# A cached page's eight chunk rows laid 16 partitions apart instead of side by side

## What is computed

```
def gather_pages(pool, page_table):
    g = pool[page_table]
    return g.reshape(page_table.shape[0], -1, 2, N_KV_HEADS, HEAD_DIM)

def compress_blocks(kv, cmp_pe, cmp_w):
    # BLOCK_CMP 32, STRIDE_CMP 16, so r = 2 and a chunk is 16 positions
    chunks = kv[:, :n_chunks * STRIDE_CMP].reshape(B, n_chunks, STRIDE_CMP, 2, N_KV_HEADS, HEAD_DIM)
    comp = 0.0
    for i in range(r):
        part = chunks[:, i:i + n_cmp] + pe[i]
        comp = comp + jnp.einsum('bnscgd,csde->bncge', part, w[:, i])
    return comp[:, :, 0], comp[:, :, 1], c_end
```

## Time and profile before

| | |
|---|---|
| median of three runs | 2737.37 us |
| lowest and highest | 2721.35 and 2755.52 us |
| the profiled execution | 2724.35 us |
| its span | 2722.6 us |
| mean granted share of TensorE's clock | 0.935 |
| PE busy | 2351.4 us, 86% of the span |
| DVE, ACT, GpSimd busy | 804.9, 559.6 and 170.2 us |
| mean rate of the DMA engines | 43 GB/s |

### The profile page before, as it was taken

How to read it: one execution, slowest core, us unless ns; L and a number is a source line. 1 busy time by engine, 2 the same in 40 slices (tenths; PEclk the granted TensorE clock), 3 DMA queues, 4 the chain that set the end, 5 groups by cost and what they waited for, 6 DMA issues and landing times.

```text
span 2722.6 us, 37448 instructions
## 1 busy us (share of the span) xinstructions
PE 2351.4 (86%) x15820; PEld 1321.1 (49%) x15820; DVE 804.9 (30%) x1750; ACT 559.6 (21%) x1292; POOL 170.2 (6%) x253
## 2 busy tenths in 40 slices
PE   8999899888874696877755589899999999999999
PEld 4464445787863573333322334454454445444543
DVE  2046333556551237765433201101110111111101
ACT  4024331222211124655512212100000000000000
POOL 2000000222201111111100000000000000000000
PEclk9998889999985897999977799899999999999999
DMA  5000003000005530000033330101011010101000
GB/s 156 17 8 23 24 16 120 3 11 11 3 4 87 98 111 1 1 1 1 23 117 109 85 141 27 62 0 62 3 59 62 0 62 0 62 0 62 0 31 35
DMA packets 84726, 115.75 MB, mean 43 GB/s; under 512 B 30899, under 2 KB 68724, under 8 KB 83406
## 3 DMA queue, kind: packets, MB, share of 16 engines
q1 hardware_dynamic: 84558, 113.35, 13.9%
HBM read 104.75 MB, written 12.64 MB: 43 GB/s over the span
## 4 chain that ended last, share of the span: by engine, by line
PE 75%; DVE 7%; DMA 5%; SPq 4%; ACT 4%; issue 3%; POOL 0%; POOLq 0%; DVEq 0%; ACTq 0%
PE psum L1121 71%; DMA arena<-in_cache_cmp_kv_dram 3%; SPq L612 2%; DVE arena L2067 2%; SPq L580 2%; PE psum L1524 1%; ACT arena L1028 1%; PE psum L1581 1%; DVE arena L1934 1%; ACT arena L1014 1%; DVE psum L2062 1%; DMA arena<-in_w_out_dram 1%; SPq L596 1%; PE psum L1461 1%; DMA arena<-in_w_up_dram 0%
## 5 line engine op out<-in xcount | busy, mean ns | idle before, releaser
L1121 PE MATMUL psum<-arena 64*64 64x64 f32 (+11 forms) x12912 | 2089.1, 353 | 177.3 <-ACT arena L1028 53.8
L1121 PEld LDWEIGHTS psum<-arena 64*64 64x64 f32 (+5 forms) x12912 | 1088.7, 156 | 1079.1 <-issue 891.3
L1115 ACT ACTIVATE arena<-psum 128x512 f32<-128x512 f32 (+1 forms) x96 | 45.4, 473 | 837.7 <-PE psum L1121 837.7
L2199 DVE TENSOR_TENSOR arena<-arena 128x512 f32<-128x512 f32 (+1 forms) x96 | 51.5, 537 | 455.9 <-ACT arena L1115 455.9
L2208 DVE TENSOR_TENSOR arena<-arena,psum 128x512 f32<-128x512 f32 (+1 forms) x72 | 49.4, 685 | 449.9 <-PE psum L1121 449.9
L1581 PE MATMUL psum<-ident,arena 128*128 128x128 f32 (+1 forms) x248 | 47.7, 337 | 80.3 <-DMA arena<-in_cache_slc_kv_dram 74.4
L731 POOL TENSOR_TENSOR arena<-arena,m_lev 128x256 f32<-128x256 f32 x82 | 67.3, 821 | 684.9 <-DVE arena L1915 440.2
L1014 ACT ACTIVATE arena<-psum 128x512 f32<-128x512 f32 (+1 forms) x148 | 80.6, 595 | 95.2 <-PE psum L1524 81.6
L1028 ACT ACTIVATE arena<-psum,arena 128x640 f32<-128x640 f32 (+7 forms) x128 | 89.6, 701 | 30.9 <-DVE arena L2067 28.8
L2067 DVE TENSOR_REDUCE arena<-psum 128x1 f32<-128x640 f32 (+7 forms) x128 | 90.6, 708 | 4.4
L1461 PE MATMUL psum<-ident,arena 128*128 128x128 f32 (+1 forms) x288 | 46.8, 293 | 46.4 <-DVE arena L2017 46.4
(11 more groups left out here) (281 smaller groups left out, 1218.1 us busy)
## 6 DMA issues: line engine op xcount, KB each, us to landing
arena<-in_cache_cmp_kv_dram SPq DMA_DIRECT2D x128, 128.0 KB
arena<-in_cache_slc_kv_dram SPq DMA_DIRECT2D x128, 128.0 KB, 2.3
arena<-in_w_down_dram SPq DMA_DIRECT2D x4, 4096.0 KB, 13.7
arena<-in_w_up_dram SPq DMA_DIRECT2D x4, 4096.0 KB, 13.6
arena<-in_x_prompt_dram SPq DMA_DIRECT2D x16, 512.0 KB, 9.4
arena<-in_w_in_dram SPq DMA_DIRECT2D x13, 512.0 KB, 3.8
arena<-in_w_in_dram SPq DMA_DIRECT2D x2, 2048.0 KB, 14.6
arena<-in_cache_win_kv_dram SPq DMA_DIRECT2D x8, 512.0 KB, 5.0
```

Of the source, the lines that this page charges most:

```text
L1121: return nc.tensor.matmul(out, lhsT, rhs, start=start, stop=stop)
```

## The change

The destination of page n's transfer is partitions n, n + 16, ..., n + 112 instead of 8n to 8n + 7 (`flat[n:P:NPG, :]`, with NPG = 16): chunk c of page n lies on partition 16c + n. The source of the transfer, its size, the number of transfers, their order and their semaphores are the same. After the transposes the columns of PSUM are therefore in the order (c, n). The copies at L992 and L2027 read a bank with its columns 16 apart for the inner index c (8 elements) and 1 apart for n (16 steps) and write `xt` contiguously, so that `xt` holds the chunks in their order again. For unit 0 the two helpers return the same elements as before. Nothing else is changed, and no instruction moves on any engine.

```diff
--- before.py
+++ after.py
@@ -331,6 +331,19 @@
             return (by_head[0:n, part].rearrange("p c s d -> p s c d"),
                     shaped(chunk_flat[u % 2][0:n], STRIDE, 2 * KVH, HD)[:, :, part, :])
 
+        def in_order(v, u):
+
+            flat = v.rearrange("p a b c -> p (a b) c")
+            if u == 0:
+                return flat[:, :, 0:SEQ // STRIDE]
+            return flat.rearrange("p a (c n) -> p a n c", n=NPG)
+
+        def xt_of(g, u):
+            flat = xt[g % 4].rearrange("p a b c -> p (a b) c")
+            if u == 0:
+                return flat[:, :, 0:SEQ // STRIDE]
+            return flat.rearrange("p a (n c) -> p a n c", n=NPG)
+
         def chunk_loads(u):
 
             return 16 * (1 + NPG * (u // 2)) if u % 2 == 0 else 16 * NPG * (u // 2 + 1)
@@ -590,10 +603,9 @@
                     sp.dma_start(flat[0:SEQ // STRIDE, :], prompt_cmp[0, 0].rearrange(
                         "n (c s) a g d -> (n c) (s a g d)", s=STRIDE)).then_inc(sem("chunk_in0"), 16)
                     return
-                rows_of_page = PAGE // STRIDE
                 for n in range(NPG):
                     src = cache_cmp_kv[0, bass.ds(at_page[n], 1)].rearrange("o (c s) a g d -> (o c) (s a g d)", s=STRIDE)
-                    sp.dma_start(flat[n * rows_of_page:(n + 1) * rows_of_page, :], src).then_inc(sem(f"chunk_in{u % 2}"), 16)
+                    sp.dma_start(flat[n:P:NPG, :], src).then_inc(sem(f"chunk_in{u % 2}"), 16)
 
             sp.wait_ge(sem("cmp_stored"), 16 * PT)
             for u in range(NSEQ):
@@ -988,9 +1000,7 @@
                     act.wait_ge(sem("cm_turned"), g + 1)
                     if g >= 4:
                         act.wait_ge(sem("cm_mm"), g - 3)
-                    n = SEQ // STRIDE if u == 0 else P
-                    nc.scalar.activation(xt[g % 4][:, :, :, 0:n], shaped(banks[g % 4], 2, KVH, P)[:, :, :, 0:n],
-                                         ACT.Copy).then_inc(sem("cm_x1"), 1)
+                    nc.scalar.activation(xt_of(g, u), in_order(shaped(banks[g % 4], 2, KVH, P), u), ACT.Copy).then_inc(sem("cm_x1"), 1)
                 ncm = NCMP_P if u == 0 else NCMP
                 act.wait_ge(sem("cm_sel"), u + 1)
                 nc.scalar.activation(kc_all[:, u, 0:ncm], banks[6][:, 0:ncm], ACT.Copy)
@@ -2024,7 +2034,7 @@
                     dve.wait_ge(sem("cm_turned"), g + 1)
                     if g >= 4:
                         dve.wait_ge(sem("cm_mm"), g - 3)
-                    nc.vector.tensor_copy(xt[g % 4][:, :, :, 0:n], shaped(banks[g % 4], 2, KVH, P)[:, :, :, 0:n]).then_inc(sem("cm_x0"), 1)
+                    nc.vector.tensor_copy(xt_of(g, u), in_order(shaped(banks[g % 4], 2, KVH, P), u)).then_inc(sem("cm_x0"), 1)
                     if f == 4 and u + 1 < NSEQ:
                         key_rows(u + 1)
                 dve.wait_ge(sem("cm_mm"), 8 * (u + 1))
```

## The result

The changed kernel takes 2750.79 us (median of 20 runs, 2742.78 to 2755.54) against 2735.06 us before (20 runs, 2713.95 to 2790.66). The medians differ by 16 us. The ratio is 1.0068, 95% interval 1.0048 to 1.0087, or about 19 us; it leaves out three runs of before that took over 1.5% more than its fastest. The kernel is slower by under 1%. The runs after lie within 13 us, those before within 77.

A forecast was written before the change was run, and what follows sets the result against it. The prediction took the page loads' shared SBUF write paths as the bound: eight loads of 20.4 us plus landing and tail end the stage 10 us later. Added to the 2737.4 us median this gave 2747 us, range 2706 to 2768.

The forecast's parts named there:

- What bounds the stage, and that its end decides: The 176 us stage loading cache_cmp_kv: loads set the pace, PE in the last third; prompt attention starts at its end.
- Rows 16 apart share paths in pairs and the rate stays level: Page transfers: eight engines, two per SBUF write path, every load at 100 to 105 GB/s, the last like the first.
- the sum: Eight loads of 20.4 us at 103 GB/s, plus landing and tail: stage ends 10 us later, time 2747 us.
- SP's part, 16.6 us a unit and so hidden behind 20.4 us of transfer: SP's pointer reads and issues take 16.6 us a unit, below a load's 20.4, so transfers in flight hide them.
- The signs that I had named: In the later profile: DMA share 0.50, loads 20 to 21 us apart, 100 to 105 GB/s, SP waiting for the copies.
- First load and tail: First load: 20.4 us plus 2.3 from issue to landing; after the last load, 21 us to the stage's end (19.9 to 22.3).
- The copies: DVE and ACT copies out of PSUM, 688 and 599 ns: unchanged to twice as long, adding 0 to 1.5 us.
- the rate of own paths: Rival, 10%: every row has its own write path or pairs part at once; SP limits, stage 29 us earlier, 2708 us.
- the source: Rival, 8%: the first loads are limited where the same eight chunks are read together; nothing changes, 2737 us.
- a path shared by four: Rival, 5%: rows 16 apart lie on two paths, four engines each; 51 GB/s, 41 us a load, 2913 us.
- The slow drift: Rival, 15%: pairs of engines drift apart slowly; mean load 18.7 us, stage ends at 1020.5, 2733 us.
- my case: The likeliest case, 60%: engines share write paths in pairs, 20.4 us a load, stage 10 us longer, 2747 us.

The follow-up runs named there:

- e3: The changed kernel (rows 16 apart) with page numbers fixed in the program instead of read from the page table; 2713.17 us, ratio 0.9892.
- e4: The changed kernel with page numbers fixed in the program and a page's rows 4 partitions apart instead of 16; 2677.58 us, ratio 0.9778.
- e6b: The changed kernel with the first three samples' page numbers read into registers earlier, while SP waits for time mixing to end; 2726.88 us, ratio 0.9969.
- e8: The kernel before, unchanged, profiled a second time; 2735.06 us.
- e1: The kernel before (neighbouring rows), with SP issuing the page transfers in the longer form that 16-apart transfers have; 2769.61 us, ratio 1.0105.
- e5: The changed kernel with rows 4 partitions apart instead of 16, page numbers still read from the page table; 2752.36 us, ratio 1.0060.

## Why the prediction was right, and where it was not

- **What bounds the stage, and that its end decides**: right for the kernel before; the time less the stage's end is 1697 to 1704 us in every profile.
- **Rows 16 apart share paths in pairs and the rate stays level**: right in part. With eight engines busy, rows 16 apart moved at 117 to 121 GB/s in e3 and rows 4 apart at 212 in e4; the last ACT copies end 38.9 us apart (at 1016.3 and 977.4). No run shows which partitions have a path in common, or at what lead engines no longer meet: the sum's "two on a path" was my estimate, and in place of its 103 GB/s the runs showed 110 to 134 with rows 16 apart and all eight engines busy. The 110 are of the changed kernel's first load. So the term of the sum was too large: 20.4 us a load, measured 18.2 in e3, where SP does not hold it, and 15.5 twice in e6b. That the rate stays what it is at first did not hold in e6b (120, then 134 GB/s); what raised it was not separated. And the level rate after the change is SP's pace, not the paths': right for another reason.
- **SP's part, 16.6 us a unit and so hidden behind 20.4 us of transfer**: this step failed. I took the issue of a transfer as unchanged because its size and number were. It went from 277 to 585 ns, 16 x 0.31 = 5 us of the 5.7 that a unit grew by, and SP's 22.3 us stand above the 20.4 of the sum and the 18.2 measured. The signs that I had named for it say the same: the share is 0.44 instead of 0.50, and SP waits for no copy. A row of mine could have warned: the issue of L590 had 0.59 us in the earlier trace rows, with 64 neighbouring rows, so a long issue was there without any distance between rows; which patterns bring one was not mapped.
- **First load and tail**: 21.4 us from issue to copy (22.7 in the sum) and 1054.7 - 1032.4 = 22.3 us of tail, where I took 21 and had 22.3 as the longer case.
- **The copies**: 688 and 599 ns as before; reading PSUM 16 columns apart cost nothing here.
- **The sum**: the stage was to take 186.5 us and took 199.2. That the time came out at 2751 for 2747 is luck. Measured against the profile that the sum started from, the stage is 23 us longer, not 10. But that profile was a fast course of the kernel before: I added the 10 us of that comparison to the median, and a run at the median (e8, 2735.06 us) has a stage of 186 us, not 176. The stage that I forecast was too short, and so was the one that I compared it with; the two errors largely cancel.
- **The rivals**: the rate of own paths, 8 x 25.6 = 205 GB/s, is not reached 16 apart (134 at most), but comes with rows 4 apart (212 in e4); the source is out (76, 117 and 212 GB/s from the same one); a path shared by four is out, since no load with rows 16 apart was near 51 GB/s (94 at least). The slow drift, with its 18.7 us a load, is nearer to e3's 18.2 than my case is, though e3 shows no climb and only e6b does.

Open: the first issue came at 848.0, 848.8 and 852.9 us before and at 855.5 and 852.9 after. Nothing ahead of it is changed, and in each the issue comes 10.1 to 10.2 us behind that of the prompt's chunks, so the difference arises earlier. With e1 (851.3, like before up to there) and e5 (853.2, like after) the two groups overlap; seven profiles do not settle whether it is chance.

## What to carry to other kernels

When a transfer's access pattern changes, look up the price of issuing it, not only of moving it. Here it went from 277 to 585 ns, sixteen issues and sixteen page reads a unit took SP 22.3 us, and that became the pace; a layout that moved at 212 GB/s brought nothing then (e5, ratio 1.0060). Place the rows of one transfer by the rate that their places reach, not by an even spread over the partitions: on eight engines 16 apart gave 110 to 134 GB/s, 4 apart 212. The kernel before scattered by 77 us over 20 runs, the changed one by 13, and the stage of the former took 176 to 208.5 us in three profiles: one profile of such a layout is one throw, so compare with a profile whose time is near the median.

## What the hardware showed that I had not expected

The issue of an 8-row transfer with its page number in a register took 277 ns on SP with neighbouring rows, 585 ns with rows 16 apart and 645 ns in e1 and with rows 4 apart. One register read of a page number with its companions took 0.58 to 0.61 us, 9.3 us a unit before and 9.8 after: more than the sixteen issues before (7.6 us), less than those after (12.4). And the same program moved its eight loads in anything from 176 to 209 us of stage, with single loads after the first between 11 and 30 us.
